# A mixer, experts and attention kernel: the last eight modulation slabs moved behind the second norm's sums, two group norms rooted on few partitions, GpSimd slab subtractions in pieces of 256 columns

## What is computed

```python
# group norms at the end of the mixer
yc = y - mean(y, over the 64 channels of a head)
yn = yc * rsqrt(mean(yc*yc, over the 64 channels) + 64e-5) * ln_w + ln_b      # RWKV half, 8 heads
og = o * rsqrt(mean(o*o, over the 128 channels of a head) + 1e-6) * g         # GLA half, 4 heads
x = x + concat([(yn + bonus) * gate, og * silu(gate2)]) @ w_out
h = rmsnorm(x, ln2_w)                 # the "second norm"; router and experts read it

# modulation vectors of the second block, both layers
ml = split(silu(c) @ w_ada[l] + b_ada[l], 9)
mc = split(silu(c_ctx) @ w_ada[l] + b_ada[l], 9)
```

## Time and profile before

| what | value |
|---|---|
| median of 3 runs | 3141.08 us (3140.27 to 3143.2) |
| the profiled execution | 3141.97 us, its span 3140.2 us |
| TensorE matmul busy | 2929.1 us, 93% of the span |
| VectorE busy | 1548.4 us, 49% |
| ScalarE busy | 1011.9 us, 32% |
| GpSimd busy | 305.7 us, 10% |
| mean granted TensorE clock | 0.965 of full speed |
| DMA | 547.83 MB, mean 174 GB/s |

### The profile page before, as it was taken

One profiled execution on the slowest core, in us unless ns is written; L12 is line 12 of the kernel. 1 busy time (PEld: TensorE's weight loads), 2 busy tenths in 40 slices (PEclk: granted clock), 3 DMA queues, 4 the chain that ended last, 5 costly groups with the idle time before them and its releaser, 6 DMA issues.

```text
span 3140.2 us, 55276 instructions
## 1 busy us (share of the span) xinstructions
PE 2929.1 (93%) x23909; PEld 2386.9 (76%) x23909; DVE 1548.4 (49%) x2226; ACT 1011.9 (32%) x1470; POOL 305.7 (10%) x223
## 2 busy tenths in 40 slices
PE   6988877899999989999899999999999998989999
PEld 6876565677767689977568878888788887769999
DVE  6534234232323366673764344444544457476666
ACT  3211113222222244532642232222322224264443
POOL 5123100000000000132100010000000003210000
PEclk9998887999999989999999999999999999999999
DMA  6346766999999945411012232222222222104652
GB/s 247 124 161 268 295 268 275 420 396 377 378 381 378 385 175 188 148 68 40 1 41 108 86 129 94 94 94 94 81 94 94 94 94 81 54 3 167 235 188 81
DMA packets 77069, 547.83 MB, mean 174 GB/s; under 512 B 8384, under 2 KB 10432, under 8 KB 11056
## 3 DMA queue, kind: packets, MB, share of 16 engines
q1 hardware_dynamic: 76000, 540.05, 44.3%
q0 software_dynamic: 848, 4.53, 0.4%
HBM read 637.87 MB, written 1.05 MB: 203 GB/s over the span
## 4 chain that ended last, share of the span: by engine, by line
PE 84%; DVE 8%; DMA 4%; ACT 2%; issue 1%; POOL 1%; DVEq 0%; POOLq 0%; SPq 0%; ACTq 0%
PE bank L764 56%; PE bank L1123 11%; DMA ring<-slabs 4%; PE bank L1473 2%; PE bank L828 1%; DVE tiny L2737 1%; PE bank L1325 1%; PE bank L1561 1%; PE bank L958 1%; PE bank L1329 1%; PE bank L945 1%; PE bank L1542 1%; PE bank L1332 1%; DVE wk L2714 1%; PE bank L1642 1%
## 5 line engine op out<-in xcount | busy, mean ns | idle before, releaser
L764 PE MATMUL bank<-hhi,whi 128*128 128x256 f32 (+1 forms) x1280 | 434.1, 339 | 0.6 <-ACT wk L1987 0.4
L764 PE MATMUL bank<-hlo,whi 128*128 128x256 f32 (+1 forms) x1280 | 432.8, 338 | 0.0
L764 PE MATMUL bank<-hhi,wlo 128*128 128x256 f32 (+1 forms) x1280 | 429.7, 336 | 0.0
L2169 DVE TENSOR_TENSOR wlo<-ring,whi 128x2048 fp32r<-128x2048 f32 x132 | 298.8, 2287 | 207.6 <-ACT whi L1674 201.9
L764 PE MATMUL bank<-fhl,whi 128*128 128x256 f32 (+1 forms) x1408 | 348.1, 339 | 0.0
L1674 ACT ACTIVATE whi<-ring 128x2048 fp32r<-128x2048 f32 x132 | 251.6, 1908 | 212.3 <-PE bank L764 212.2
L1123 PE MATMUL bank<-ring,wk 128*32 128x256 f32 x4064 | 254.9, 394 | 21.3 <-DMA ring<-slabs 13.0
L764 PEld LDWEIGHTS bank<-hhi,wlo 128*128 128x128 f32 x1280 | 243.1, 190 | 28.9
L764 PEld LDWEIGHTS bank<-fhl,whi 128*128 128x128 f32 x1408 | 240.3, 188 | 32.0
L764 PEld LDWEIGHTS bank<-hhi,whi 128*128 128x128 f32 x1280 | 239.9, 187 | 30.1 <-issue 1.8
L764 PEld LDWEIGHTS bank<-hlo,whi 128*128 128x128 f32 x1280 | 240.4, 188 | 27.8
(11 more groups left out here) (493 smaller groups left out, 5605.5 us busy)
## 6 DMA issues: line engine op xcount, KB each, us to landing
ring<-slabs SPq DMA_DIRECT2D x542, 1024.0 KB
wk<-slabs SPq DMA_DIRECT2D x45, 1024.0 KB, 12.5
ac<-slabs SPq DMA_DIRECT2D x16, 1024.0 KB, 12.1
wk<-mixp POOLq DMA_DIRECT2D x1, 1040.0 KB, 12.6
xt<-xT SPq DMA_DIRECT2D x1, 1024.0 KB, 6.9
xt<-ctxT POOLq DMA_DIRECT2D x1, 1024.0 KB, 6.0
out<-xt SPq DMA_DIRECT2D x4, 256.0 KB, 2.4
cst<-maskc POOLq DMA_DIRECT2D x1, 960.0 KB, 14.6
```

The lines of the kernel that those rows point to most:

```text
L764: last = pe.matmul(o, a, b, start=k == 0, stop=k == len(pairs) - 1)
L2169: tt_(wlo_of(n), slab(n), whi_of(rel).bitcast(F32), ALU.subtract).then_inc(sem("wlo"), 1)
```

## The change

1. Of the 72 modulation slabs the last eight (`N_LATE`, one half group, number 64 to 71) are stored and multiplied after the four `w_out` slabs: `ada(N_LATE)` stands directly behind the sums of the second norm. Their turn (`ada_t`) stands between the two router products.
2. The other slabs stand elsewhere: 10 instead of 16 in the GLA part, 4 instead of 8 behind its state products, 4 at a new place behind the spread of the first root, 6 ahead of `mixr`.
3. Both group norms at the end of the mixer take their root and reciprocal on 32 x 64 and 16 x 64 instead of 128 x 1024. Gathering and spreading are matmuls of 64 columns; VectorE then multiplies straight from PSUM.
4. `SROW` moves to the upper half of `rs`, the sums of the second norm go to bank 5, and two constants grow (78 columns more of `small`).
5. Each of the 26 GpSimd subtractions of 128 x 2048 is issued as eight of 128 x 256.

```diff
-S_WOUT = S_ADA + N_ADA
-S_MOE = S_WOUT + 4
+N_LATE = 8
+S_WOUT = S_ADA + N_ADA - N_LATE
+S_MOE = S_ADA + N_ADA + 4
+def ada_slab(n):
+    return S_ADA + n + (4 if n >= N_ADA - N_LATE else 0)
-ADA_PREP, ADA_MAT, ADA_GLA, ADA_GMAT = 12, 1, 16, 8
+ADA_PREP, ADA_MAT, ADA_GLA, ADA_GMAT, ADA_NORM = 12, 1, 10, 4, 4
...
# GpSimd
-                    pool.tensor_tensor(wlo_of(n), slab(n), att_whi(l, i).bitcast(F32), ALU.subtract
-                                       ).then_inc(sem("al"), 1)
+                    for q in range(0, SLAB, FB):
+                        c = slice(q, q + FB)
+                        ins = pool.tensor_tensor(wlo_of(n)[:, c], slab(n)[:, c], att_whi(l, i)[:, c].bitcast(F32),
+                                                 ALU.subtract)
+                    ins.then_inc(sem("al"), 1)
...
# TensorE
             pe.wait_ge(sem("ysq"), 1)
-            for j in range(4):
-                mm = pe.matmul(b3(2 + j // 2, 2)[:, j % 2, :], BO64, SQM[:, j, :], start=True, stop=True)
+            for r in range(16):
+                mm = pe.matmul(bank[2][0:32, 0:RCOL], pc("eblk", 30 - 2 * r, 32),
+                               SQM[:, r // 4, r % 4 * RCOL:(r % 4 + 1) * RCOL], start=r == 0, stop=r == 15)
...
+            pe.wait_ge(sem("yvr"), count("yvr", 1))
+            for r in range(32):
+                part, c = slice(r % 2 * 64, r % 2 * 64 + 64), r // 2 % 8 * RCOL
+                mm = pe.matmul(bank[2 + r // 16][part, c:c + RCOL], IDENT[0:32, r:r + 1].to_broadcast([32, 64]),
+                               YVR, start=True, stop=True)
+            mm.then_inc(sem("yvb"), 1)
+            ada(ADA_NORM)
             pe.wait_ge(sem("gsq"), 1)
-            for j in range(4):
-                mm = pe.matmul(b3(2 + j // 2, 2)[:, j % 2, :], O128, SQM[:, j, :], start=True, stop=True)
+            for r in range(16):
+                mm = pe.matmul(bank[6][0:16, 384:384 + RCOL], pc("erow", 15 - r, 16),
+                               SQM[:, r // 4, r % 4 * RCOL:(r % 4 + 1) * RCOL], start=r == 0, stop=r == 15)
             mm.then_inc(sem("gss"), 1)
-            ada(N_ADA - ada_n[0])
+            pe.wait_ge(sem("yvc"), count("yvc", 1))
+            pe.wait_ge(sem("gsr"), count("gsr", 1))
+            for r in range(16):
+                mm = pe.matmul(bank[2 + r // 8][:, r % 8 * RCOL:(r % 8 + 1) * RCOL],
+                               IDENT[0:16, r:r + 1].to_broadcast([16, P]), GSR, start=r % 8 == 0, stop=r % 8 == 7)
+            mm.then_inc(sem("gsb"), 1)
+            ada(N_ADA - N_LATE - ada_n[0])
...
+            pe.wait_ge(sem("adr"), N_ADG - 1)
             norm(1, TX)
+            ada(N_LATE)
             pe.wait_ge(sem("hn"), 16)
...
+                if tt == 0:
+                    ada_t(N_ADG - 1)
+            pe.wait_ge(sem("modc"), N_ADG)
...
# ScalarE
-            for h in range(2):
-                ins = act.activation(RSM[:, 2 * h:2 * h + 2, :], b3(2 + h, 2), ACT.Sqrt, bias=pc("eps", 1))
-            ins.then_inc(sem("yvd"), 1)
+            act.activation(YVR, bank[2][0:32, 0:RCOL], ACT.Sqrt, bias=pc("eps", 1)[0:32, :]).then_inc(sem("yvd"), 1)
...
# VectorE
             dve.wait_ge(sem("yvd"), 1)
-            then(dve.reciprocal(RSM, RSM))
-            then(tt_(CEN, CEN, RSM, ALU.mult))
+            dve.reciprocal(YVR, YVR).then_inc(sem("yvr"), 1)
+            dve.wait_ge(sem("yvb"), count("yvb", 1))
+            for h in range(2):
+                ins = tt_(CEN[:, 2 * h:2 * h + 2, :], CEN[:, 2 * h:2 * h + 2, :], b3(2 + h, 2), ALU.mult)
...
+            dve.wait_ge(sem("gssd"), 1)
+            dve.reciprocal(GSR, GSR).then_inc(sem("gsr"), 1)
...
-            then(dve.reciprocal(RSG, RSG))
-            then(tt_(OT, OT, RSG, ALU.mult))
+            dve.wait_ge(sem("gsb"), count("gsb", 1))
+            for h in range(2):
+                ins = tt_(OT[:, 2 * h:2 * h + 2, :], OT[:, 2 * h:2 * h + 2, :], b3(2 + h, 2), ALU.mult)
```

More of the change, by code:

```diff
@@ L773, in norm @@
                     pe.wait_ge(sem("sq"), KT * n + j + 1)
-                    mm = pe.matmul(bank[7][:, 0:T], O1024, AC[:, j, 0:T], start=j == 0, stop=j == KT - 1)
+                    mm = pe.matmul(bank[NORM_BANK[n]][:, 0:T], O1024, AC[:, j, 0:T], start=j == 0, stop=j == KT - 1)
                 mm.then_inc(sem("ss"), 1)
@@ L786, in root_rows @@
                     for c in range(rows):
-                        mm = pe.matmul(bank[3][0:rows, 0:RCOL], pc("erow", 7 - c, rows), HT[:, j, c * RCOL:(c + 1) * RCOL],
+                        mm = pe.matmul(bank[3][0:rows, 0:RCOL], pc("erow", 15 - c, rows), HT[:, j, c * RCOL:(c + 1) * RCOL],
                                        start=j == tiles[0] and c == 0, stop=j == 7 and c == rows - 1)
@@ L824, in ada @@
                     last = i == ADA_G - 1 or n == N_ADA - 1
-                    s = slab(S_ADA + n).rearrange("p (k c) -> p k c", k=KT)
+                    s = slab(ada_slab(n)).rearrange("p (k c) -> p k c", k=KT)
                     for k in range(KT):
@@ L1863, in _ @@
             act.wait_ge(sem("yv"), 1)
-            for h in range(2):
-                ins = act.activation(RSM[:, 2 * h:2 * h + 2, :], b3(2 + h, 2), ACT.Sqrt, bias=pc("eps", 1))
-            ins.then_inc(sem("yvd"), 1)
+            act.activation(YVR, bank[2][0:32, 0:RCOL], ACT.Sqrt, bias=pc("eps", 1)[0:32, :]).then_inc(sem("yvd"), 1)
             act.activation(SQM, OT, ACT.Square).then_inc(sem("gsq"), 1)
             act.wait_ge(sem("gss"), 1)
-            for h in range(2):
-                ins = act.activation(RSG[:, 2 * h:2 * h + 2, :], b3(2 + h, 2), ACT.Sqrt, bias=pc("eps", 0))
-            ins.then_inc(sem("gssd"), 1)
-            ada(N_ADA - ada_n[0])
+            act.activation(GSR, bank[6][0:16, 384:384 + RCOL], ACT.Sqrt, bias=pc("eps", 0)[0:16, :], scale=D / P
+                           ).then_inc(sem("gssd"), 1)
+            ada(ADA_NORM)
+            ada(N_ADA - N_LATE - ada_n[0])
             norm(1, TX)
+            ada(N_LATE)
             act.wait_ge(sem("rx"), count("rx", 1))
@@ L2992, in _small @@
     put("eps", np.array([[RMS_EPS, GN_EPS, 1.0]]))
-    put("erow", np.eye(1, 15, 7) / D)
+    put("erow", np.eye(1, 31, 15) / D)
+    put("eblk", np.repeat(np.eye(2, 62, 30), 64, 0) / 64)
     return out
```

25 lines of the change are left out of this document (15 added, 10 removed).

## The result

| | median us | lowest to highest | ratio to before, 95% |
|---|---|---|---|
| before | 3140.68 (4 runs) | 3137.93 to 3143.2 | |
| changed | 3098.34 (4 runs) | 3091.81 to 3100.51 | 0.9862 [0.9849, 0.9875] |
| changed, run again (e1_after) | 3096.17 (5 runs) | 3092.1 to 3105.28 | 0.9854 [0.9841, 0.9868] |

The change gives 42 to 45 us. The profiled execution took 3100.51 us, its span 3098.7.

What follows compares the result with a forecast made beforehand. TensorE, busy 93% of the span, was taken as the bound, with waits in the mixer and attentions. From 3141.97 us, mixer -24.4 and attentions -8.8 gave 3108.8, or 3108 at the median; range for 8 in 10: 3098 to 3123.

Steps and rivals of the forecast that it cites:

- The GLA part: Mixer: with ten slabs, transposes wait for VectorE instead of slabs, and products 1061 start 20.4 us earlier (bounds 17 and 22).
- the 3.4 that would have made 17: GLA part, lower bound: all 9.2 us of work at half clock for a third more leaves 17 us gained.
- The roots: Mixer, products 1061 to `w_out`: removing 13 us of reciprocals, mostly eaten by added records and slabs, gains 0.8 us.
- `w_out`: Mixer: slabs directly ahead keep the clock up, so its first 12 records gain 2.1 us (bounds 0 and 2.1).
- Late slabs and router: Second norm's sums to router products: eight slabs fill the wait, the router runs at full clock; 1.1 us gained.
- The mixer: GLA part, roots, `w_out`, late slabs and router together: 24.4 us gained, within 14 and 27.
- Attentions: GpSimd pieces: 12.0 us gained in waits for VectorE, 3.2 paid for longer slabs; net -8.8, bounds -14 and +7.
- Rival 1: Attentions: VectorE isn't let in between pieces, so these cost +3 to +12; total 3122 us, chance 0.10.
- rival 3: Attentions: GpSimd pays at every seam; above 1.55 us a piece TensorE waits, 3166 us at 1.9; chance 0.04.
- The constants: Whole kernel: the wider constants, 40 KB more, cost about 0.1 us.
- The experts: Expert stage: first slabs are requested later, but idle DMA time absorbs the backlog; cost 0, bound 8 us.

Runs made afterwards that it cites:

- e2_sched: The changed kernel with roots, constants and GpSimd subtractions as before, so only the modulation slabs moved: 3122.97 us, ratio 0.994 to the kernel before.
- e1_pieces: The kernel before with only the GpSimd attention subtractions cut into eight instructions of 256 columns: 3132.24 us, ratio 0.9972.
- e2_pad: The kernel before with 78 unused columns in the tile of constants, so later tiles lie 320 bytes higher: 3131.45 us, ratio 0.997.
- e4_back: The changed kernel with 16 unused columns more in the tile of constants (384 bytes in all): 3101.2 us, ratio 0.9867 to the kernel before.
- e3_extra: The kernel before with 72 small unused matmuls added on TensorE right ahead of `w_out`: 3140.45 us, ratio 1.0001.
- e1_mixer: The changed kernel with the GpSimd pieces undone, so modulation slabs and norm roots alone: 3105.64 us, ratio 0.9892 to the kernel before.

## Why the prediction was wrong

**The GLA part: right.** 19.5 us for 20.4. The transposes waited for VectorE and began where foreseen (369.84 less the late start of 2.87 is 367.0), and the work up to the next slabs took 5.8 us instead of 5.0, 3.77 of it for 32 records at a granted clock of 0.51 (before they took 2.20 us). The products 1073 came 0.8 us later than foreseen, not the 3.4 that would have made 17. The Trainium skill, TensorE: Matmul & The Clock Gate, "Why this matters for your kernels", warns of the lower clock behind idle gaps. The trace agrees for these records, behind 6.09 us of idle time.

**The roots: right that they are worth little, by errors that cancel.** The first spread took 2.08 us instead of 3.9 (0.032 each). My reason, that neighbouring matmuls use different halves of the array, is not shown: its weights also have 64 columns instead of 128, and no run separates the two. The second spread took 4.93 us instead of 3.7 and the six slabs 7.48 instead of 5.3, because the sum had them at the full clock and the granted one was 0.74 and 0.71. From the products to `w_out` 38.7 us, forecast 37.9, before 38.7. Without the roots, in e2_sched, that stretch is even shorter, 37.5 us. What the roots bring comes behind it. From the start of `w_out` to the sums of the second norm 29.2 us pass (418.59 to 447.80) instead of 31.6 in e2_sched (417.64 to 449.21), because TensorE comes from slabs and not from 8.9 us of idling. Another 1.2 us lie behind the sums. In all that is 2.3 us for the most intricate part of the change; their constants and their instructions bought more.

**`w_out`: right** (2.1 both). **Late slabs and router: right** (0.9, forecast 1.1). The mixer measured 21.3 by the mean of the profiles, 22.5 by the first pair, for 24.4.

**Attentions: right.** -8.8 forecast, -8.8 timed in e1_pieces, 10.3 in its profile. The terms came out too: the waits for VectorE fell by 10.5 us (17.0 to 6.5), as in the sum, and those for GpSimd's low parts rose by 2.9 (1.7 to 4.6) for 3.2. Rival 1 fell: VectorE is let in after a piece, and its longest instruction on the lines that had been stretched is 0.95 us. A piece took 758 ns, a slab 6.1 us (I took 6.4), so rival 3's point of 1.55 us a piece was far.

The Trainium skill, SBUF — State Buffer, "Who interferes with whom", calls the ports that VectorE and GpSimd share an exclusive lock. It says that a VectorE instruction with two SBUF inputs contends for them with a GpSimd instruction that reads SBUF, and of VectorE's two-port modes that whoever issues first has the pair for the whole instruction. The rows agree for the two-input instructions (0.42 against 4.58 us), and the cure follows: what is held is held for an instruction, so the instruction has to be short. What happens between two instructions that section leaves open; here VectorE gets in.

**The failed steps** are two that I set at nothing.
- *"The constants (40 KB more) cost about 0.1."* I priced their transfer and not what lies behind them. They move every later tile by 320 bytes. In the changed kernel that makes the 1488 matmuls of each long feed-forward 3.05 us shorter, 6.1 together. In the kernel before it alone is 9 us by the time (e2_pad), and another shift by 64 bytes takes back 4.5 of the 6.1 (e4_back). No row of the trace of before could have shown it, but the edit to the tile's width was in the diff.
- *"The experts ... Cost 0, bound 8 us."* I bounded a loss by late slabs and no gain. The stage became 6.3 us shorter, 4.7 of which are gaps marked issue that stood in the traces of before (11.0 us in the second). TensorE waits in them for the next block of its instructions, and a shift of its stream by 72 matmuls changes them in the same way (e3_extra).

The two errors have one sign and together are the missing 10 us. By the profiles, 33.2 forecast, plus 6.3 in the experts, 6.1 by the place and 1.6 in the attentions, less 3.1 that the mixer fell short, is 44, for 42 to 45 timed. That the time came out within a microsecond of the range's end is luck: the range was meant for other errors.

Two differences of the table look like the change and are the clock. The start of the span is 3.5 us longer in the changed kernel's two profiles, in which the lower clock level was granted for 54.6 and 61.4 us of it, against 47.7 and 51.2 before. It goes with that time in kernels of either kind (347.5 us with 47.7 in e1_mixer, 350.4 with 54.6 in e2_sched). Layer 1's second feed-forward is 379.7 us in the changed kernel and 376.92 in e1_mixer, at the same pace. The lower level was granted for 10.2 us of it in the one and for 3.4 in the other. It shows at the end of this stretch, in the sums of the next norm. The changed kernel, then e1_mixer:

```profile
2193.13 4.47 PE L801 MATMUL bank<-ht,par 128*8 128x64 f32 x48 [1.96 <-POOL ht L739]
```

```profile
2194.86 2.85 PE L798 MATMUL bank<-ht,par 128*8 128x64 f32 x48 [1.96 <-POOL ht L739]
```

The granted clock was 0.63 in the first and 1.00 in the second. Whether the pieces have a part in this no run shows.

What stays open is why the place of the tiles sets the pace, and where the 3 us lie by which e2_pad's time gained more than its long feed-forwards.

## What to carry to other kernels

Price every line of a diff that moves something else: a wider constant tile moves all tiles behind it, and added instructions move all later ones in their queue. Where a gain turns up in a stage that the change doesn't touch, pad the old kernel with unused columns, or with unused instructions, before explaining it; the two paddings cost a line or two each and here explained most of 10 us. Compare the granted clock of the stage too, before a difference of 3 us is put down to an edit. And where one engine locks another out by a long instruction, cutting it pays as long as the pieces together stay inside their slack.

## What the runs showed of the hardware

- The pace of 512-column matmuls depends on the place of their tiles in SBUF at an equal granted clock of 1.00. From start to start it is 232.5 ns at the old place (1488 in 345.72 us), 230.4 at 64 and 320 bytes more (342.67), and 232.0 at 128 and 384 (344.91).
- Groups of 128 records of two columns are followed by gaps of up to 4.8 us in which nothing visible is waited for, and their sum over a stage changes from 11 to 6 us with 72 matmuls put in front. Each of the 108 gaps over 0.4 us marked issue, in the 17 traces, ends 1.2 to 1.6 us behind the end of a 16384-byte transfer of the instruction queue.
- The median GpSimd subtraction of 128 x 256 takes 735 ns, of 128 x 512 1293 and of 128 x 2048 4611: 0.18 us beside 0.56 for every 256 columns fits all three. The means of the pieces are higher (758 and 1334), since some are longer (up to 931 and 1525 ns). VectorE gets in between two of them.
- A spread by matmuls of 32 x 64 weights that alternate between halves of the array took 0.032 us a record at a granted clock of 1.00. With 16 x 128 weights it was 0.15 at 0.74 and 0.22 at 0.50.
